# Modulation loads and matmuls in the norm holes of a two-block mixer stack: one unit between the sums and their spreading, eleven units instead of eight behind the mixers

## The chip, the cores and the metric

The kernel runs on one core of a Trainium2 chip. The metric is the device time of one execution in microseconds (us); the time before is the median of three runs. TensorE is called PE, VectorE DVE, ScalarE ACT, GpSimd POOL and SyncE SP.

## What is computed

A stack of two blocks over 256 tokens of width 1024, two layers each, all in float32. Only the parts that the change touches are shown. A layer of the first block is

```python
m = mixer_block(rms_norm(x, norm_mix_pre[layer]), ...)
x = x + rms_norm(m, norm_mix_post[layer])
h = rms_norm(x, norm_ffn_pre[layer])
f = swiglu(h, w_ffn_gate[layer], w_ffn_up[layer], w_ffn_down[layer])
x = x + rms_norm(f, norm_ffn_post[layer])
```

The second block is modulated: for each of its two layers a vector of 6 x 1024 numbers is needed for the latents and another for the context,

```python
mod_x = jax.nn.silu(c) @ ada_w[l] + ada_b[l]
mod_c = jax.nn.silu(c_ctx) @ ada_w[l] + ada_b[l]
```

with `ada_w[l]` of 1024 x 6144. These products depend on nothing that the first block makes, and the kernel computes them while the first block runs.

## The kernel before, in words

**The weight stream.** All weights lie in HBM as units of 128 x 1024 floats (512 KB). SP loads the units of the matrices one after the other into three buffers `raw` (L906, after waiting for `lo_ready` of the unit three before); ACT makes the rounded high part `w_hi` of each unit (L1492) and POOL the rest `w_lo` (L945, two halves), each in four buffers; PE multiplies by both. Products run tile by tile: `product` (L987 to L989), `product_halves` (L1003, L1007) and, for the first two tiles of a stage, `side_by_side` (L1047 to L1050), which takes row tile k of both as soon as `h_ready` tells of row k.

**The modulation units.** `ada_w` of both layers is 96 units of 512 KB, numbered 0 to 95, 48 for each layer. A unit is loaded by `load_modulation` on SP (L915) into one of six buffers (`ADA_SLOTS`), which lie in parts of `spare_lo`, `mix` and `spare_hi` that the first block leaves free. Its load waits for `ada_used` of the unit six before. On PE `modulation_unit` (L1141 to L1153) waits for the unit's load (`ada_loaded`) and does four products of 128 x 2 by 128 x 256 (L1151, eight matmul records, since a float32 product takes two). `ada_places` says at which of the places of a layer of the first block the units stand: at certain tiles of the gates and branches, in the feed-forward part (`FFNS`, 22 pairs of tiles), and in the norms: `MID1` and `PRE1` between the mixer and the feed-forward part, `MID2` and `PRE2` behind the feed-forward part of layer 0. Layer 0 of the first block carries units 0 to 47, layer 1 units 48 to 95. Before the change `MID1` has units 16 to 21 and `PRE1` units 22 and 23 in layer 0, and 68 to 73 and 74, 75 in layer 1.

**The order of the loads.** One list, `LOADS`, built by `load_order`, holds the loads of both kinds for SP's one queue. A modulation load stands where the unit six before it is used. Behind the mixer of layer 0 the list runs: raw units 80 to 90, modulation units 22 to 29, raw unit 91; in layer 1: raw units 233 to 241, modulation units 74 to 81, raw unit 242.

**The norm holes.** Behind the last product of the mixer (`product(y1, 0, SEQ)`) come two norms. `last_rows_sum` sums the squares of the mixer's output over the width on PE (L1090), ACT takes the root (L1544), DVE the reciprocal (L1933), and `spread_inverse` spreads the result over the partitions on PE (L1103, waits for `inv_ready`). DVE then scales and adds to `xs` tile by tile (L2040, L2044), ACT squares each tile (L1521), and `norm_sums` sums these on PE (L1090), again with root, reciprocal and spreading. DVE and ACT then make the normed rows `hl` (L1942, L1550, L1946), and `side_by_side` starts the feed-forward part. In `norm_sums` the units of `MID1` stand as follows: all but three ahead of the sums, and one each behind the sums of tiles 1, 3 and 5. The units of `PRE1` stand behind the spreading.

PE runs its instructions in the order of the program, SP its own likewise: a wait on either holds back all that stands behind it.

Of the kernel before, what the change touches and what calls it, by code (L numbers as in the profile page):

```python
# [19 lines left out]
DEPTH = 2  # L20
# [8 lines left out]
NFF = FF // P  # L29
# [24 lines left out]
POST1, MID1, PRE1 = 3 * KD, 3 * KD + 1, 3 * KD + 2  # L54
FFNS = list(range(3 * KD + 3, 3 * KD + 3 + NFF))
POST2, MID2, PRE2 = FFNS[-1] + 1, FFNS[-1] + 2, FFNS[-1] + 3
# [3 lines left out]
def spread(n, places):  # L60
    out, groups = [0] * N_PLACES, -(-n // ADA_GROUP)
    for i in range(n):
        out[places[i // ADA_GROUP * len(places) // groups]] += 1
    return out


def ada_places(l):

    counts = spread(16 if l < DEPTH - 1 else 20, GATES[4:])
    for place, n in ((MID1, 6), (PRE1, 2)):  # L70
        counts[place] += n
    for place, n in enumerate(spread(16 if l < DEPTH - 1 else 20, FFNS[3:NFF - 3])):
        counts[place] += n
    if l < DEPTH - 1:
        counts[MID2] += 6
        counts[PRE2] += 2
    assert sum(counts) == ADA_LAYER
    at, n = [], l * ADA_LAYER
    for more in counts:
        at.append(list(range(n, n + more)))  # L80
        n += more
    return at


ADA_AT = [ada_places(_l) for _l in range(DEPTH)]
ROWS_AT, TURN_AT, MOD_AT = {}, {}, {}
for _l in range(DEPTH):
# [384 lines left out]
SINGLE1, SINGLE2 = 1, 3  # L472
# [80 lines left out]
def mixer_stack_kernel(nc, stream, vectors, consts, decay, gla_masks, positions, x_in, ctx_in, out):  # L553
# [186 lines left out]
    STAT, X = banks[2], banks[3:8]  # L740
# [150 lines left out]
    with nc.Block() as block:  # L891
# [65 lines left out]
        def _(pe):  # L957
# [13 lines left out]
            def product(x, c0, c1, count=1, fresh=None, late=None, more=1):  # L971

                for i_tile in range(count):
                    t, n, b = TILES[at["tile"]], PLACE.first_out[at["tile"]], PLACE.first_block[at["tile"]]
                    acc = bank_of(n)[:, c0:c1]
                    for k in range(t.k):
                        wait_unit((b + k) // UNIT)  # L980
                        slot, i = (b + k) // UNIT % SPLIT, (b + k) % UNIT
                        wh, wl = w_hi[:, slot, i * P:(i + 1) * P], w_lo[:, slot, i * P:(i + 1) * P]
                        if late and late[1] == k:
                            E.need(late[0])
                        if fresh and i_tile == 0:
                            E.need(fresh, more)
                        nc.tensor.matmul(acc, wh, x[:, 0, k, c0:c1], start=k == 0, stop=False)  # L987
                        nc.tensor.matmul(acc, wh, x[:, 1, k, c0:c1], start=False, stop=False)  # L988
                        last = nc.tensor.matmul(acc, wl, x[:, 0, k, c0:c1], start=False, stop=k == t.k - 1)  # L989
                        if k == t.k - 1:  # L990
                            last.then_inc(tile_done, 1)
                        elif i == UNIT - 1:
                            last.then_inc(unit_used, 1)
                    at["tile"] += 1
# [33 lines left out]
            def keep_busy(acc, count):  # L1028

                for _ in range(count):  # L1030
                    nc.tensor.matmul(acc[:, 0:2 * P], ident, cst[:, 0:2 * P], start=True, stop=True)
# [55 lines left out]
            def token_sums(bank, row, c0, c1, first, last):  # L1087

                for j in range(c0 // P, c1 // P):
                    done = nc.tensor.matmul(bank[:, j * P:(j + 1) * P], row[:, j * P:(j + 1) * P], ones,  # L1090
                                            start=first and j == c0 // P, stop=last, skip_group_check=True)
                return done

            def stat_free():
                if at["stat"]:
                    E.need(std_ready)
                at["stat"] += 1

            def spread_inverse(bank, c0, c1):

                E.need(inv_ready)
                for j in range(c0 // P, c1 // P):
                    last = nc.tensor.matmul(bank[:, j * P:(j + 1) * P], inv_col[:, j:j + 1].to_broadcast([P, P]), ident,  # L1103
                                            start=True, stop=True)
                last.then_inc(inv_spread, 1)

            def last_rows_sum(c0, c1, single):

                E.need(sq_ready)
                stat_free()  # L1110
                token_sums(STAT, work[:, 0, :], c0, c1, True, False)
                for k in range(KD - single, KD):
                    E.need(sq_tile, 1 if k > KD - single else KD - single + 1)
                    last = token_sums(STAT, work[:, k, :], c0, c1, False, k == KD - 1)
                last.then_inc(stat_ready, 1)
                spread_inverse(STAT, c0, c1)

            def norm_sums(c0, c1, bank, units=(), spread_bank=None, spare=0):
                stat_free()
                keep_busy(bank, spare)  # L1120
                for unit in units[:-3]:
                    modulation_unit(unit)
                for k in range(KD):
                    E.need(sq_ready)
                    last = token_sums(bank, work[:, k, :], c0, c1, k == 0, k == KD - 1)
                    if k % 2 and k // 2 < len(units[-3:]):
                        modulation_unit(units[-3:][k // 2])
                last.then_inc(stat_ready, 1)
                spread_inverse(spread_bank or bank, c0, c1)

            def projected(x, l, c0, fresh, next_norm, more=1):

                if l == DEPTH - 1:
                    product_halves(x, c0, T2, KD - 1, fresh=fresh, more=more)
                    product(x, c0, T2)
                else:
                    product(x, c0, T2, KD, fresh=fresh, more=more)
                if next_norm:
                    last_rows_sum(c0, T2, SINGLE2)

            def modulation_unit(unit):  # L1141

                part, k, slot = unit // KD, unit % KD, unit % ADA_SLOTS
                acc = X[1 + part % 3]
                pe.wait_ge(ada_loaded[slot], 16 * (unit // ADA_SLOTS + 1))
                if unit == 0:
                    pe.wait_ge(silu_c_ready, 1)
                if k == 0 and part >= 3:
                    pe.wait_ge(ada_rows_out, part - 2)
                for j in range(4):  # L1150
                    last = nc.tensor.matmul(acc[32 * j:32 * j + 2, 0:ADA_COLS], silu_c[:, k, :], ada_raw[slot][:, j, :],  # L1151
                                            start=k == 0, stop=k == KD - 1)
                last.then_inc(ada_used, 1)  # L1153
# [11 lines left out]
            def modulation_at(l, place):  # L1165
                for unit in ADA_AT[l][place]:
                    modulation_unit(unit)
                if (l, place) in TURN_AT:
                    turn_modulation(TURN_AT[l, place])
# [2 lines left out]
            pe.wait_ge(ones_loaded, 16)  # L1172
            c0, c1 = LAT
            for l in range(DEPTH):
                norm_sums(c0, c1, X[4], ADA_AT[l - 1][MID2] if l else ())
                if l:
                    modulation_at(l - 1, PRE2)
                pe.wait_ge(cst_loaded, 16)
                outs = {}
                for step, i in MIX1:  # L1180
                    if step in ("g", "r", "c", "rg", "gr"):
                        n = {"g": 5, "r": 2, "c": 3, "rg": RH, "gr": GH}[step]
# [6 lines left out]
                    elif step == "diag" or step == "take":  # L1189
# [8 lines left out]
                        for h, j in [(h, j) for i_pair in range(2) for j in range(2) for h in (2 * i_pair, 2 * i_pair + 1)]:  # L1198
# [4 lines left out]
                            k = gqk[rows, 1, h // 2, :] if step == "diag" else k_dec[rows, h // 2, :]  # L1203
                            if step == "take" and i == 0:
                                c, k, q = h // 2 * P, k[:, 0:P], q[:, P:SEQ]
                            else:
                                c, k, q = (h // 2 * 2 + j) * P, k[:, j * P:(j + 1) * P], q[:, j * P:(j + 1) * P]
# [16 lines left out]
                    elif step == "score":  # L1224
                        q, k = rqk[:, i, 0, :], rqk[:, i, 1, :]
# [44 lines left out]
                        modulation_at(l, KD * b + f)  # L1270
                product_halves(y1, 0, SEQ, KD - 1, fresh=merged_ready)
                product(y1, 0, SEQ)
                last_rows_sum(c0, c1, SINGLE1)
                norm_sums(c0, c1, X[4], ADA_AT[l][MID1])
                modulation_at(l, PRE1)
                for t in range(NFF):
                    if t:
# [9 lines left out]
                product(hid, 0, SEQ)  # L1287
                if l == DEPTH - 1:
                    pe.wait_ge(ctx_root, 1)
                last_rows_sum(c0, c1, SINGLE1)  # L1290


            for l in range(DEPTH):
                c0 = 0 if l < DEPTH - 1 else SEQ
# [6 lines left out]
                for step, i in mixer2(l):  # L1301
# [52 lines left out]
                    elif step == "att":  # L1354
# [14 lines left out]
                        if 2 <= i < len(pairs) + 2:  # L1369
                            n = before + i - 2  # L1370
# [60 lines left out]
                    elif step == "acc":  # L1431
                        h, d, n = i
# [1208 lines left out]
```

## Time and profile before

| | |
|---|---|
| median of three runs | 2741.41 us (2739.74 to 2745.48) |
| the profiled execution's own time | 2744.02 us |
| its span (first to last instruction) | 2741.8 us |
| granted TensorE clock, mean | 0.993 |
| PE busy, matmuls | 2661.7 us (97%) |
| PE busy, weight loads | 2272.6 us (83%) |
| DVE, ACT, POOL busy | 1315.5, 1286.7, 1608.9 us |
| HBM read | 382.51 MB, 140 GB/s over the span |

The profiled execution's own time is 2.2 us more than its span, for what lies around the first and the last instruction, and 2.6 us more than the median. A timeline row has its start and its length in us, the engine, the line, the operation, what it writes and reads, how many instructions are merged in it, and in brackets the idle time ahead of it with what ended that. The ends of matmuls are modelled and overlap the next one's start; the pitch from start to start is what PE takes. SPq rows are SP's issues of DMAs, not the transfers. In a view of windows the last three columns are the granted clock as a share of 2.4 GHz, the mean busy share of the 16 DMA engines, and the bytes moved per second.

### The profile page before, as it was taken

The numbers are of one execution on the slowest core, as the hardware profiler recorded it, in microseconds if no ns is written. First come the engines' busy times: TensorE is split into PE (matmuls) and PEld (weight loads), VectorE is DVE, ScalarE is ACT, GpSimd is POOL, SyncE is SP. The second block draws the span as 40 slices with busy tenths as digits, with TensorE's granted clock in tenths as the row PEclk, the third lists the DMA queues.
The fourth block names the chain that finished last, engine by engine and source line by source line (L and its number), as shares of the span: only waits on it lengthen the run. The fifth ranks groups of instructions, "written<-read, shape, count | busy, mean of one in ns | idle before, by whom it ended". The sixth has DMA issues, their size and how long they took to land.

```text
span 2741.8 us, 41593 instructions
## 1 busy us (share of the span) xinstructions
PE 2661.7 (97%) x16136; PEld 2272.6 (83%) x16136; DVE 1315.5 (48%) x2433; ACT 1286.7 (47%) x2042; POOL 1608.9 (59%) x1252
## 2 busy tenths in 40 slices
PE   7999999999999999999999999999999999999999
PEld 7898788888887888786788788888887889998888
DVE  4575533256654343875523424432333855335644
ACT  5464544444645454436434333442343565445644
POOL 5678688767786885432233345444443635457787
PEclk9999999999999999999999999999999999999999
DMA  5357776534686753221121222233222423234455
GB/s 204 116 192 269 230 253 225 162 122 139 229 294 223 261 171 128 82 81 47 52 79 62 77 85 96 81 100 100 93 93 80 143 85 116 93 108 160 158 181 162
DMA packets 144867, 386.12 MB, mean 141 GB/s; under 512 B 11824, under 2 KB 64304, under 8 KB 144688
## 3 DMA queue, kind: packets, MB, share of 16 engines
q1 hardware_dynamic: 144688, 383.61, 42.5%
q8 instruction: 128, 2.10, 0.3%
q14 instruction: 51, 0.42, 0.1%
HBM read 382.51 MB, written 1.05 MB: 140 GB/s over the span
## 4 chain that ended last, share of the span: by engine, by line
POOL 52%; issue 46%; PE 1%; POOLq 1%; DMA 0%; DVE 0%; ACT 0%; DVEq 0%
POOL w_lo L945 52%; PE bank L1003 1%; POOLq L942 0%; PE bank L1007 0%; DMA raw<-stream 0%; POOLq L949 0%; PE bank L989 0%; PE bank L988 0%; PE bank L987 0%; POOLq L945 0%; ACT fc L1903 0%; DVE fc L2591 0%; DVE xs L2326 0%; DVE bank L2603 0%; DVE hid L2606 0%
## 5 line engine op out<-in xcount | busy, mean ns | idle before, releaser
L945 POOL TENSOR_TENSOR w_lo<-raw,w_hi 128x512 fp32r<-128x512 f32 x1248 | 1608.7, 1319 | 1123.0 <-ACT w_hi L1492 1120.4
L1492 ACT ACTIVATE w_hi<-raw 128x1024 fp32r<-128x1024 f32 x624 | 655.0, 1054 | 379.9 <-DMA raw<-stream 170.3
L987 PE MATMUL bank<-hl,w_hi 128*128 128x512 f32 (+1 forms) x2016 | 694.0, 344 | 15.7 <-POOL w_lo L945 11.2
L989 PE MATMUL bank<-hl,w_lo 128*128 128x512 f32 (+1 forms) x2016 | 677.8, 336 | 0.0
L988 PE MATMUL bank<-hl,w_hi 128*128 128x512 f32 (+1 forms) x2016 | 677.7, 336 | 0.0
L987 PEld LDWEIGHTS bank<-hl,w_hi 128*128 128x128 f32 x2016 | 387.3, 192 | 62.7 <-issue 10.3
L988 PEld LDWEIGHTS bank<-hl,w_hi 128*128 128x128 f32 x2016 | 387.6, 192 | 42.0 <-issue 4.4
L989 PEld LDWEIGHTS bank<-hl,w_lo 128*128 128x128 f32 x2016 | 387.1, 192 | 38.3
L1003 PE MATMUL bank<-hl,w_hi 128*128 128x512 f32 x1312 | 344.1, 395 | 2.2 <-POOL w_lo L945 1.9
L1003 PEld LDWEIGHTS bank<-hl,w_hi 128*128 128x128 f32 x1312 | 234.7, 189 | 50.2 <-issue 9.0
L1007 PEld LDWEIGHTS bank<-hl,w_lo 128*128 128x128 f32 x1312 | 181.5, 190 | 16.2 <-DVE hl L2566 2.9
L1007 PE MATMUL bank<-hl,w_lo 128*128 128x256 f32 x1312 | 186.5, 282 | 2.2 <-DVE hl L2566 2.2
L2591 DVE SCALAR_TENSOR_TENSOR fc<-bank,vec,fc 128x510 f32<-128x510 f32 (+1 forms) x88 | 54.2, 616 | 182.2 <-ACT fc L1903 182.1
L2326 DVE SCALAR_TENSOR_TENSOR xs<-bank,mod,xs 128x256 f32<-128x256 f32 x93 | 42.8, 481 | 180.4 <-PE bank L989 132.8
L1003 PE MATMUL bank<-hid,w_hi 128*128 128x512 f32 x462 | 128.0, 397 | 0.0
L1903 ACT ACTIVATE fc<-bank,vec 128x512 f32<-128x512 f32 (+1 forms) x88 | 59.0, 671 | 138.2 <-PE bank L989 108.8
L2381 DVE SCALAR_TENSOR_TENSOR bank<-z,vec,bank 128x512 f32<-128x512 f32 (+1 forms) x232 | 123.0, 612 | 0.0
L1070 PE MATMUL bank<-w_hi,hl 128*128 128x256 f32 x384 | 111.7, 291 | 5.4 <-POOL w_lo L945 5.3
L987 PE MATMUL bank<-y,w_hi 128*128 128x256 f32 (+1 forms) x336 | 110.6, 329 | 2.1 <-DVE y L2560 1.8
L1071 PE MATMUL bank<-w_lo,hl 128*128 128x256 f32 x384 | 109.2, 284 | 0.0
L1072 PE MATMUL bank<-w_hi,hl 128*128 128x256 f32 x384 | 109.2, 284 | 0.0
L989 PE MATMUL bank<-y,w_lo 128*128 128x256 f32 (+1 forms) x336 | 108.7, 324 | 0.0
(327 smaller groups left out, 3998.3 us busy)
## 6 DMA issues: line engine op xcount, KB each, us to landing
raw<-stream SPq DMA_DIRECT2D x624, 512.0 KB, 3.4
spare_lo<-stream SPq DMA_DIRECT2D x32, 512.0 KB, 5.8
mix<-stream SPq DMA_DIRECT2D x32, 512.0 KB, 5.9
spare_hi<-stream SPq DMA_DIRECT2D x32, 512.0 KB, 5.8
xs<-x_rows SPq DMA_DIRECT2D x4, 256.0 KB, 4.1
xs<-ctx_rows SPq DMA_DIRECT2D x1, 1024.0 KB, 14.5
out_rows<-xs SPq DMA_DIRECT2D x8, 128.0 KB, 2.8
dec<-decay SPq DMA_DIRECT2D x1, 768.0 KB, 11.0
```

The source lines that it names most:

```text
L945: last = nc.gpsimd.tensor_tensor(w_lo[:, unit % SPLIT, part], raw[:, unit % RAW, part], w_hi[:, unit % SPLIT, part], ALU.subtract)
L987: nc.tensor.matmul(acc, wh, x[:, 0, k, c0:c1], start=k == 0, stop=False)
L988: nc.tensor.matmul(acc, wh, x[:, 1, k, c0:c1], start=False, stop=False)
L989: last = nc.tensor.matmul(acc, wl, x[:, 0, k, c0:c1], start=False, stop=k == t.k - 1)
L1003: return nc.tensor.matmul(acc[:, :], w, x[:, :, k, c0:c1], start=k == 0, stop=k == t.k - 1)
L1007: return nc.tensor.matmul(acc[:, 0:SEQ], w, x[:, 0, k, c0:c1], start=False, stop=False)
L1070: nc.tensor.matmul(acc, h_hi[:, k, c:c + P], wh, start=k == 0, stop=False)
L1071: nc.tensor.matmul(acc, h_hi[:, k, c:c + P], wl, start=False, stop=False)
L1072: last = nc.tensor.matmul(acc, h_lo[:, k, c:c + P], wh, start=False, stop=k == t.k - 1)
L1492: nc.scalar.activation(w_hi[:, n % SPLIT, :], raw[:, n % RAW, :], ACT.Copy).then_inc(hi_ready, 1)
L1903: nc.scalar.activation(fc[:, t % 2, j, cols], rows, ACT.Identity, bias=v_("ffn_conv_b_2", l, i), scale=v_("ffn_conv_w_2", l, 2 * NFF + i)) ...
L2381: C.do(V.scalar_tensor_tensor(out, z, w, y, MUL, ADD))
```

## The change

The places `MID1` and `PRE1` get eight and three units instead of six and two, and the last places of the feed-forward part three fewer in each layer. One unit of `MID1` (and of `MID2`) moves up into `last_rows_sum`, between the sums and the spreading; one of them moves behind the last sum of `norm_sums`, again between the sums and the spreading. Three units still stand between the sums of `norm_sums`, the rest ahead of them.

```diff
@@ def ada_places(l):
     counts = spread(16 if l < DEPTH - 1 else 20, GATES[4:])
-    for place, n in ((MID1, 6), (PRE1, 2)):
+    for place, n in ((MID1, 8), (PRE1, 3)):
         counts[place] += n
-    for place, n in enumerate(spread(16 if l < DEPTH - 1 else 20, FFNS[3:NFF - 3])):
+    for place, n in enumerate(spread(13 if l < DEPTH - 1 else 17, FFNS[3:NFF - 3])):
         counts[place] += n
@@
-            def last_rows_sum(c0, c1, single):
+            def last_rows_sum(c0, c1, single, units=()):
...
                 last.then_inc(stat_ready, 1)
+                for unit in units:
+                    modulation_unit(unit)
                 spread_inverse(STAT, c0, c1)
 
             def norm_sums(c0, c1, bank, units=(), spread_bank=None, spare=0):
                 stat_free()
                 keep_busy(bank, spare)
-                for unit in units[:-3]:
+                for unit in units[:-4]:
                     modulation_unit(unit)
                 for k in range(KD):
                     E.need(sq_ready)
                     last = token_sums(bank, work[:, k, :], c0, c1, k == 0, k == KD - 1)
-                    if k % 2 and k // 2 < len(units[-3:]):
-                        modulation_unit(units[-3:][k // 2])
+                    if k % 2 and k // 2 < len(units[-4:-1]):
+                        modulation_unit(units[-4:-1][k // 2])
                 last.then_inc(stat_ready, 1)
+                for unit in units[-1:]:
+                    modulation_unit(unit)
                 spread_inverse(spread_bank or bank, c0, c1)
@@
-                norm_sums(c0, c1, X[4], ADA_AT[l - 1][MID2] if l else ())
+                norm_sums(c0, c1, X[4], ADA_AT[l - 1][MID2][1:] if l else ())
@@
-                last_rows_sum(c0, c1, SINGLE1)
-                norm_sums(c0, c1, X[4], ADA_AT[l][MID1])
+                last_rows_sum(c0, c1, SINGLE1, ADA_AT[l][MID1][:1])
+                norm_sums(c0, c1, X[4], ADA_AT[l][MID1][1:])
                 modulation_at(l, PRE1)
@@
-                last_rows_sum(c0, c1, SINGLE1)
+                last_rows_sum(c0, c1, SINGLE1, ADA_AT[l][MID2][:1])
```

By the same functions the units then stand so. Layer 0: `MID1` has units 16 to 23 (16 in `last_rows_sum`, 17 to 19 ahead of the sums, 20, 21 and 22 between them, 23 behind them) and `PRE1` units 24 to 26; the group of four at the 16th pair of feed-forward tiles shrinks to one unit (39). Layer 1: `MID1` has 68 to 75, `PRE1` 76 to 78, and the last group is unit 95 alone. The list of loads has modulation units 22 to 32 between raw units 90 and 91, and 74 to 84 between raw units 241 and 242. `MID2` keeps units 40 to 45: 40 in `last_rows_sum`, 41 ahead, 42 to 44 between, 45 behind.

## Rows read from the trace of the kernel before

**Rows 1.** The page: busy time by engine, and the chain that ended last

```profile
PE 2661.7 (97%) x16136; PEld 2272.6 (83%) x16136; DVE 1315.5 (48%) x2433; ACT 1286.7 (47%) x2042; POOL 1608.9 (59%) x1252
...
POOL 52%; issue 46%; PE 1%; POOLq 1%; DMA 0%; DVE 0%; ACT 0%; DVEq 0%
```

**Rows 2.** Timeline of PE, norm holes behind the mixer, layer 0

```profile
318.14 1.35 PE L1090 MATMUL bank<-cst,work 128*128 128x128 f32 x8
320.04 0.71 PE L1103 MATMUL bank<-cst,sd 128*128 128x128 f32 x4 [0.55 <-DVE sd L1933]
320.68 1.04 PE L1151 MATMUL bank<-spare_hi,silu_c 128*2 128x256 f32 x16
...
327.14 0.61 PE L1151 MATMUL bank<-mix,silu_c 128*2 128x256 f32 x8
327.69 1.16 PE L1090 MATMUL bank<-cst,work 128*128 128x128 f32 x8
329.46 0.71 PE L1103 MATMUL bank<-cst,sd 128*128 128x128 f32 x4 [0.62 <-DVE sd L1933]
330.10 1.04 PE L1151 MATMUL bank<-spare_hi,silu_c 128*2 128x256 f32 x16
332.07 0.47 PE L1048 MATMUL bank<-hl,w_hi 128*128 128x512 f32 x1 [0.92 <-DVE hl L1946]
```

**Rows 3.** Timeline of PE, a group of four units, feed-forward part of layer 0

```profile
428.23 1.04 PE L1151 MATMUL bank<-spare_lo,silu_c 128*2 128x256 f32 x16
429.10 1.05 PE L1151 MATMUL bank<-mix,silu_c 128*2 128x256 f32 x16
```

**Rows 4.** Timeline of SP's issues around the norm holes, layer 0

```profile
302.55 19.53 SPq L906 DMA_DIRECT2D raw<-stream  x8
322.12 1.22 SPq L915 DMA_DIRECT2D spare_hi<-stream  x2
323.39 1.70 SPq L915 DMA_DIRECT2D spare_lo<-stream  x2
326.18 2.17 SPq L915 DMA_DIRECT2D mix<-stream  x2
```

**Rows 5.** DMA issues in windows at 322.12, 323.39 and 326.18: us to landing

```profile
spare_hi<-stream SPq DMA_DIRECT2D x1, 512.0 KB, 5.7
...
spare_lo<-stream SPq DMA_DIRECT2D x1, 512.0 KB, 8.8
...
mix<-stream SPq DMA_DIRECT2D x1, 512.0 KB, 9.0
```

**Rows 6.** Timeline of PE, the same holes, layer 1

```profile
850.78 0.61 PE L1151 MATMUL bank<-spare_lo,silu_c 128*2 128x256 f32 x8
...
853.10 0.71 PE L1103 MATMUL bank<-cst,sd 128*128 128x128 f32 x4 [0.62 <-DVE sd L1933]
...
855.75 0.47 PE L1048 MATMUL bank<-hl,w_hi 128*128 128x512 f32 x1 [0.96 <-DVE hl L1946]
```

**Rows 7.** Timeline of SP's issues, layer 1

```profile
845.00 1.22 SPq L915 DMA_DIRECT2D mix<-stream  x2
...
849.82 2.17 SPq L915 DMA_DIRECT2D spare_lo<-stream  x2
```

**Rows 8.** DMA issues in windows at 845.00 and 849.82: us to landing

```profile
mix<-stream SPq DMA_DIRECT2D x1, 512.0 KB, 6.6
...
spare_lo<-stream SPq DMA_DIRECT2D x1, 512.0 KB, 7.8
```

**Rows 9.** Windows: busy of PE, PEld, DVE, ACT, POOL; PEclk, DMA share, GB/s

```profile
324.00:327.50 3.50, 3.50 (x40) 2.15 (x32) 2.70 (x8) 2.00 (x5) 0.00 (x0) 1.00 0.82 228
...
328.00:337.00 9.00, 7.46 (x56) 5.99 (x55) 6.07 (x17) 4.97 (x11) 0.41 (x1) 1.00 1.09 355
...
588.00:595.00 7.00, 4.95 (x31) 4.66 (x28) 6.83 (x8) 2.64 (x6) 6.69 (x4) 0.77 0.24 76
```

**Rows 10.** Timeline of PE: the gap ahead of the clock's fall

```profile
591.84 0.58 PE L1070 MATMUL bank<-w_hi,hl 128*128 128x256 f32 x1 [2.05 <-POOL w_lo L945]
```

## The prediction

> **What bounds the kernel now.** First the page: PE is busy 97% of the span, and the chain that ended last runs over POOL and issue [rows 1], which is an average over stages and says nothing of the one that changes. So I read the timeline of PE from the mixer's last sums to the first feed-forward matmul. In layer 0 PE stands still at four places that the rows show or imply: 0.55 us ahead of the first spreading, 0.62 us ahead of the second, both for DVE's reciprocal, 0.92 us ahead of the feed-forward part for the first normed rows, and a shorter one ahead of the second sums [rows 2]. Layer 1 looks the same, 0.62 and 0.96 us [rows 6]. Everywhere else around the change PE is in a row of matmuls without a gap: in the feed-forward part the group of four units stands between products, and what it takes is paid in full [rows 3]. So this stage is PE's, and the holes are DVE's and ACT's.
>
> Then SP's issues and their landings, since the moved units have loads that move with them. Behind the mixer raw loads go out until 302.55 + 19.53 = 322.08, then modulation units 22 and 23, from 323.39 units 24 and 25, from 326.18 units 26 and 27 [rows 4]. Unit 22 lands 5.7 us after its issue, at 327.8; unit 24 8.8 us after, at 332.2; unit 26 9.0 us after, at 335.2 [rows 5]. In layer 1 unit 74 goes out at 845.00 and lands at 851.6, unit 78 at 849.82 and lands at 857.6 [rows 7, 8]. These transfers are slow because they queue: from 328 to 337 the DMA engines are busy all the time and move 355 GB/s [rows 9], so a load of 524 KB takes 1.48 us of them.
>
> **The change part by part.**
>
> *Three units fewer in the feed-forward part of each layer.* Two units start 0.87 us before the next two [rows 3]: 0.435 us a unit. The group shrinks from four to one, so 3 x 0.435 = 1.31 us a layer, 2.61 us in all, paid in full because PE has no gap there. The group stays, and with it what it costs to go from products to units and back.
>
> *A unit between the mixer's sums and their spreading.* The hole is 0.55 us by the modelled end of the sums [rows 2]. The unit fills 0.435 us of it, and unit and spreading change over in about 0.1 us (a unit's start at 327.14 to the next sums at 327.69 is 0.55 us [rows 2]). It just fits: cost 0. It was loaded long before (its load waits for a unit used in the gates). If the cover fails it costs up to 0.435 us.
>
> *A unit behind the second sums.* The hole is 0.62 us [rows 2, 6], the same fit, cost 0 by PE. The same holds for the two holes behind layer 0's feed-forward part, where six units are only put elsewhere: 0, bound 0.435 us each.
>
> *The third unit in PRE1.* The hole ahead of the feed-forward part is 0.92 us [rows 2], so by PE it costs 0 too.
>
> *The loads.* This is the term that decides. Of the eleven units only six are loaded before the hole. Before, the two units loaded inside it (22, 23) stood at 330.10, behind the second spreading. Now units 22 to 26 are loaded inside it and all used before the feed-forward part. That unit 16 is used earlier brings nothing forward: unit 22's issue at 322.12 stands directly behind a raw load [rows 4]. Units 25 and 26 do go out earlier, some 0.6 and 1.7 us, since the units six before them are used sooner, but they queue behind 22 to 24.
> - Unit 22 is wanted at 327.14 and lands at 327.8: the sums of the last two tiles start 0.7 us late. In layer 1 unit 74 is wanted at 850.78 and lands at 851.6, 0.8 us late [rows 6 to 8]. Both are covered by what follows.
> - Unit 24 is wanted at 330.8 (the spreading at 330.2 by then) and lands at 332.2; 26 lands at 335.2. PE has then one unit left, 0.435 us, and some 0.15 us of wait and changeover, so the feed-forward part starts at 335.75 instead of 332.07: 3.7 us late. All eight normed rows are then ready or nearly so, which gives back 0.1 us: 3.6.
> - Layer 1: unit 78 lands at 857.6, the part starts at 858.2 instead of 855.75: 2.45 us late, 2.35 with what is given back.
> - The DMA engines are busy 0.82 of 324 to 327.5 [rows 9]; if the earlier issues filled all the rest, 0.18 x 3.5 = 0.6 us would be won in each layer. I take half, 0.3 each, between the ends 0 and 0.6, as the packets already queued should fill most of it.
>
> So the waits cost 3.6 + 2.35 - 0.6 = 5.35 us. Their lower end, if no load were late, is 0.
>
> A rule speaks for a cheaper wait. The row has 355 GB/s. The Trainium skill, "DMA: Bandwidth & Descriptors", section Bandwidth, has 425 GB/s for large reads from HBM with one core busy, and its Specifications put line rate at pieces of 512 bytes and up. By it a load would take an estimated 1.23 us, units 26 and 78 would land near 332.8 and 856.5, and the change would come out at about -0.2 us instead. This case's trace disagrees for these loads, and I go by it.
>
> *Queued behind the waits.* On PE the whole feed-forward part. On SP the loads of units 27 to 32 and then raw unit 91, which now stands behind three more modulation loads, 3 x 1.48 = 4.4 us of transfer. PE's own start is 3.7 us later, and raw 91 is wanted only at the fourth pair of tiles; I take 0, and up to 1 us if ACT and POOL then run late.
>
> **Sum.** -2.61 + 5.35 = +2.7 us. The profiled execution took 2744.02 us and would take 2746.7; its span of 2741.8 would be 2744.5. It lies 2.6 us over the median, so the median goes from 2741.41 to 2744.1, 0.1% slower. A measurement of this kernel tells 0.2%, 5.5 us, from no change, and not less.
>
> **Rivals.**
>
> *A, the loads come in time.* If landings follow the issues and not the queue, the five loads are there when wanted. For it: they are issued sooner, and other modulation loads land in less (5.7 us for unit 22). Against it: the engines' share of 1.09 from 328 on [rows 9], and unit 24, issued at 323.39 in both kernels, lands at 332.2 in any case. Time: -2.6 us, 2738.8; with only layer 1's loads in time about 2741.7.
>
> *B, slower: the clock falls in the stall.* In the hole of layer 0 PE would wait three times between 330.6 and 335.2, up to 1.5 us each, with units of 0.435 us between. Elsewhere in this trace a gap of 2.05 us [rows 10] stands beside a window of 7 us with a granted clock of 0.77 [rows 9]: (1 - 0.77) / 0.5 x 7 = 3.2 us at 1.2 instead of 2.4 GHz, 1.6 us lost. Against it: no single wait reaches 2.05 us, and the clock is 1.00 in both windows of layer 0 now [rows 9]. If it falls in both layers the sum is 2.7 + 3.2 = +5.9 us, 2747.3; twice as long a stretch in each gives +9.1, 2750.5. It decides from the point where PE's stall is seen with a granted clock under 1.
>
> *C, the units between sums and spreading aren't covered.* The margins are about 0.1 us. Where the DMAs rule (the second sums of both layers) it doesn't matter; at the other four holes it costs up to 4 x 0.435 = 1.7 us: +4.4, 2745.8. It is also how the change could fail to do what it says, to fill idle time.
>
> **How the numbers follow.** Forecast 55%, A 24%, B 10%, C 8%, something else 3%. The range goes from A, less 1 us for the spread of medians, to between the two sizes of B: 2737.8 to 2748.8. Faster by over 0.2% needs more than A gives: 4%. Slower by over 0.2% is B and a sum of C, late raw loads and the upper end of the waits: 13%. The rest, 83%, is within 0.2%.
>
> **What would show it.** Right: in the timeline of PE, units 24 to 26 (and 76 to 78) apart from each other by over 1 us each, with idle time ended by DMA, the first L1048 at about 335.5 and 858, and groups of one unit at the last feed-forward place; the issue-to-landing of units 24 to 26 still near 9 us; the spreading at 320.0 unmoved. Wrong: L1048 at 332 with no DMA wait (A), a granted clock under 1 in 330 to 345 (B), the first spreading later than 320.1 (C), or a new wait for POOL in the first four pairs of the feed-forward part (raw 91).

## The result, and the profile after

| | before | changed |
|---|---|---|
| median | 2742.89 us (12 runs) | 2745.95 us (12 runs) |
| lowest to highest | 2739.74 to 2745.48 | 2741.3 to 2750.36 |
| ratio, 95% interval | | 1.0016 (1.0009 to 1.0024) |

By the ratio the changed kernel is 0.16% slower, 4.4 us, with an interval of 2.5 to 6.6 us; the two medians of the table differ by 3.1 us. The forecast was 2744.1 us, 0.10% slower, and most likely too little to tell from no change. The time lies in the range of the forecast, and the direction is the forecast's. The loss stays under the 0.2% that the forecast took as the least that can be told from nothing, but the interval of these twelve runs excludes 1, so it is told all the same. The profiled execution happened to be the fastest of the twelve (2741.3 us, span 2739.1), so its span says nothing against the one of before; what follows compares stretches, not spans.

The page of the changed kernel, busy time and chain, against [rows 1]:

```profile
PE 2661.8 (97%) x16136; PEld 2269.9 (83%) x16136; DVE 1320.4 (48%) x2433; ACT 1285.6 (47%) x2042; POOL 1610.1 (59%) x1252
...
POOL 49%; issue 45%; PE 4%; POOLq 1%; DVE 1%; ACT 0%; DMA 0%; DVEq 0%; ACTq 0%
```

The same work, as it must be; the page as a whole can't show a change of this size. The timeline of PE, changed kernel, behind the mixer of layer 0, answers to [rows 2] (L1155 is `modulation_unit`, L1151 before):

```profile
318.72 1.35 PE L1090 MATMUL bank<-cst,work 128*128 128x128 f32 x8
320.62 0.71 PE L1103 MATMUL bank<-cst,sd 128*128 128x128 f32 x4
...
327.71 0.61 PE L1155 MATMUL bank<-spare_hi,silu_c 128*2 128x256 f32 x8
328.25 1.16 PE L1090 MATMUL bank<-cst,work 128*128 128x128 f32 x8
329.34 0.61 PE L1155 MATMUL bank<-spare_hi,silu_c 128*2 128x256 f32 x8
330.03 0.71 PE L1103 MATMUL bank<-cst,sd 128*128 128x128 f32 x4
330.91 0.61 PE L1155 MATMUL bank<-spare_lo,silu_c 128*2 128x256 f32 x8 [0.17 <-DMA spare_lo<-stream]
332.43 0.61 PE L1155 MATMUL bank<-spare_lo,silu_c 128*2 128x256 f32 x8 [0.91 <-DMA spare_lo<-stream]
333.92 0.61 PE L1155 MATMUL bank<-mix,silu_c 128*2 128x256 f32 x8 [0.88 <-DMA mix<-stream]
334.47 0.50 PE L1048 MATMUL bank<-hl,w_hi 128*128 128x512 f32 x1
```

Read it from the start of the sums. The first spreading stands 320.62 - 318.72 = 1.90 us behind, as before (320.04 - 318.14), the second 11.31 us against 11.32: the two new units there are covered. Then units 24, 25 and 26 come one by one, 1.5 us apart, each ended by a DMA. The first feed-forward matmul stands 15.75 us behind the sums instead of 13.93. Layer 1, same view, against [rows 6]:

```profile
855.63 0.61 PE L1155 MATMUL bank<-spare_hi,silu_c 128*2 128x256 f32 x8 [0.86 <-DMA spare_hi<-stream]
857.56 0.65 PE L1155 MATMUL bank<-spare_lo,silu_c 128*2 128x256 f32 x8 [1.31 <-DMA spare_lo<-stream]
858.14 0.79 PE L1048 MATMUL bank<-hl,w_hi 128*128 128x512 f32 x1
858.73 0.41 PE L1050 MATMUL bank<-hl,w_lo 128*128 128x256 f32 x1
```

The sums start at 842.17 here: 15.97 us instead of 13.97. The last two rows show a second thing. L1048 takes 0.79 us where [rows 2] have 0.47, and L1050 0.41 us, where it took 0.28 before. In windows of the changed and then of the old kernel (columns as in [rows 9]):

```profile
855.00:867.00 12.00, 10.05 (x60) 8.03 (x61) 6.97 (x19) 6.40 (x12) 2.52 (x2) 0.86 1.02 332
```

```profile
855.00:867.00 12.00, 11.25 (x64) 9.93 (x65) 7.49 (x19) 8.39 (x14) 6.10 (x5) 1.00 0.64 205
```

The granted clock is 0.86 instead of 1.00: (1 - 0.86) / 0.5 x 12 = 3.4 us at 1.2 GHz, right behind the stall. That is rival B, in one layer.

SP's issues and the landing of the last load, changed kernel, against [rows 4, 5] (unit 26 in the third row, its landing in the last):

```profile
321.50 1.22 SPq L915 DMA_DIRECT2D spare_hi<-stream  x2
322.76 1.40 SPq L915 DMA_DIRECT2D spare_lo<-stream  x2
325.12 2.65 SPq L915 DMA_DIRECT2D mix<-stream  x2
```

```profile
mix<-stream SPq DMA_DIRECT2D x1, 512.0 KB, 8.8
```

It goes out at 325.12, 6.40 us behind the sums instead of 8.04, and lands 8.8 us later, at 333.9, which is when PE's unit begins. Unit 22 goes out earlier as well in this execution, 321.50 - 318.72 = 2.78 us behind the sums instead of 3.98. The group at the last feed-forward place is one unit now, against [rows 3]:

```profile
430.68 0.61 PE L1155 MATMUL bank<-mix,silu_c 128*2 128x256 f32 x8
431.22 0.50 PE L1003 MATMUL bank<-hl,w_hi 128*128 128x512 f32 x1
```

### The profile page after: what moved, and what is told of

Its sections match the earlier page's. It is cut to its first block, busy times and chain, and to the rows that moved or that the text cites. A ratio compares the mean times of both kernels' runs of the same rounds, so it can differ in the third digit from the quotient of the medians.

```text
span 2739.1 us, 41594 instructions
## 1 busy us (share of the span) xinstructions
PE 2661.8 (97%) x16136; PEld 2269.9 (83%) x16136; DVE 1320.4 (48%) x2433; ACT 1285.6 (47%) x2042; POOL 1610.1 (59%) x1252
## 4 chain that ended last, share of the span: by engine, by line
POOL 49%; issue 45%; PE 4%; POOLq 1%; DVE 1%; ACT 0%; DMA 0%; DVEq 0%; ACTq 0%
POOL w_lo L945 49%; PE bank L1003 3%; PE bank L1007 1%; POOLq L942 0%; ACT fc L1907 0%; DVE fc L2595 0%; ACT w_hi L1496 0%; DMA raw<-stream 0%; POOLq L949 0%; DVE bank L2588 0%; PE bank L989 0%; PE bank L988 0%; PE bank L987 0%; DVE bank L2607 0%; DVE fc L2597 0%
## 6 DMA issues: line engine op xcount, KB each, us to landing
xs<-ctx_rows SPq DMA_DIRECT2D x1, 1024.0 KB, 14.2
```

## The experiments

A measurement tells some 0.1% here, 2 to 3.5 us, and the terms are of that size. So each run was read in two ways: the ratio, and four stretches of its one profiled execution, each the difference of two starts in the timeline of PE, within 0.01 us. A **hole** runs from the mixer's last sums (L1090 x8) to the first L1048; a **feed-forward part** from there to the next L1090. The column "sum" adds the four differences to the kernel before, in us. The last column says where a stretch at half clock begins and how long it is. Each ratio is to the kernel before in the same comparison. The line numbers of a kernel with added lines are one to three higher.

| kernel | holes, layers 0, 1 | feed-forward, 0, 1 | sum | ratio (95%) | half clock behind a hole |
|---|---|---|---|---|---|
| before | 13.93, 13.97 | 193.65, 197.60 | 0 | 1 | none |
| changed | 15.75, 15.97 | 192.42, 197.37 | +2.4 | 1.0016 (1.0009 to 1.0024) | 858.0, 3.4 us |
| e5, changed again | 16.64, 17.23 | 192.34, 198.19 | +5.3 | 1.0022 (1.0013 to 1.0031) | 857.8, 6.8 us |
| e12, changed, third | 16.82, 17.12 | 192.40, 198.18 | +5.4 | 1.0020 (1.0011 to 1.0030) | 860.7, 6.8 us |
| e1, order alone | 13.93, 13.92 | 193.66, 197.59 | 0.0 | 1.0004 (0.9994 to 1.0014) | none |
| e2, nine units | 13.92, 13.92 | 193.17, 196.83 | -1.3 | 1.0002 (0.9991 to 1.0013) | none |
| e4, five loads left out | 13.95, 13.92 | 192.33, 195.86 | -3.1 | 0.9996 (0.9986 to 1.0005) | none |
| e6, thirteen units | 20.76, 19.84 | 193.56, 195.98 | +11.0 | 1.0032 (1.0020 to 1.0044) | 340.3 and 866.0, 6.8 us each |
| e7, filled with three | 17.47, 17.95 | 192.41, 195.61 | +4.3 | 1.0013 (1.0004 to 1.0022) | none |
| e10, filled with one | 17.80, 16.77 | 192.37, 195.92 | +3.7 | 1.0004 (0.9993 to 1.0015) | none |
| e3, loads earlier | 14.01, 13.92 | 192.43, 195.89 | -2.9 | 0.9998 (0.9985 to 1.0011) | none |
| e8, the same again | 14.13, 13.92 | 192.32, 195.85 | -2.9 | 0.9997 (0.9988 to 1.0006) | none |
| e11, the same, third | 13.92, 15.88 | 192.34, 199.46 | +2.5 | 0.9985 (0.9975 to 0.9996) | none (one at 1033.4) |

**e1: the order alone.** The changed code with the old numbers:

```diff
-    for place, n in ((MID1, 8), (PRE1, 3)):
+    for place, n in ((MID1, 6), (PRE1, 2)):
-    for place, n in enumerate(spread(13 if l < DEPTH - 1 else 17, FFNS[3:NFF - 3])):
+    for place, n in enumerate(spread(16 if l < DEPTH - 1 else 20, FFNS[3:NFF - 3])):
```

> The changed order (one unit between the sums and the spreading of each norm, the rest as changed) with the old numbers: six units in MID1, two in PRE1, sixteen and twenty in the feed-forward parts. Theory W (the change loses by waits for modulation loads in the hole, and the new places of the units cost nothing): the stretch from the mixer's last sums to the first L1048 matmul stays at 13.9 us in both layers, the first spreading stays 1.90 us behind the start of the sums, and the time is that of the kernel before within 1 us (ratio 0.9997 to 1.0004). Rival C (units between sums and spreading aren't covered): each spreading 0.1 to 0.4 us later, and up to 2 us longer in all.

All four stretches are those of before within 0.05 us, and the spreadings stand at 1.90 and 11.32 us. The two holes behind the feed-forward part of layer 0 are unmoved too: from the sums there to the first product of the next mixer it is 13.92 us before, 13.92 in e1 and 13.93 in the changed kernel. Units between sums and spreading cost nothing, and alone bring nothing either. Rival C is out.

**e2: nine units.** `MID1` seven, `PRE1` two, fifteen and nineteen in the feed-forward parts.

> The changed order with nine units in the hole: seven in MID1, two in PRE1, fifteen and nineteen in the feed-forward parts. Theory W: the last unit of the hole is the third that is loaded inside it, which lands about when it is wanted (at most 0.3 us late), so the stretch from sums to first L1048 is 13.9 to 14.3 us, one unit less is paid in each feed-forward part, 0.87 us in all, and the time is 0.3 to 0.9 us under the kernel before (ratio 0.9996 to 1.0000). If what slows the changed kernel lies elsewhere than in the fourth and fifth of these loads, it is still 1 us or more over.

No wait for a load in the hole, and 0.48 and 0.77 us less in the feed-forward parts: -1.3 us in the stretches. Its ratio of 1.0002 can't be told from 1, nor from the 0.9996 to 1.0000 expected. So the loss begins with the tenth and the eleventh unit.

**e4: the loads left out.** It leaves out the loads of units 22 to 26 and 74 to 78; these units multiply by old data.

```diff
+UNLOADED = [u for l in range(DEPTH) for u in (ADA_AT[l][MID1] + ADA_AT[l][PRE1])[ADA_SLOTS:]]
...
             def load_modulation(unit):
+                if unit in UNLOADED:
+                    return
...
-                pe.wait_ge(ada_loaded[slot], 16 * (unit // ADA_SLOTS + 1))
+                pe.wait_ge(ada_loaded[slot], 16 * len([u for u in range(slot, unit + 1, ADA_SLOTS) if u not in UNLOADED]))
```

> The changed kernel without the loads of the five units that are used inside the hole beyond the six buffers (22 to 26 and 74 to 78): they are left out, and these units multiply by what the buffer holds from the unit six before, so the modulation is not the reference's. Nothing else is changed. Theory W: PE has no wait for a load in the hole, the stretch from sums to first L1048 is 13.9 to 14.0 us, and the time is the kernel before less the three units a layer, -2.6 us (ratio 0.9988 to 0.9993). Rival C: 0.4 to 1.7 us of it is lost at the spreadings. Rival B (the clock falls): with no stall no fall at 320 to 345 or 855 to 870. If the kernel stays above the one before, the loads are not the cause.

The timeline of PE of this kernel, end of the hole of layer 0:

```profile
332.40 0.71 PE L1106 MATMUL bank<-cst,sd 128*128 128x128 f32 x4
333.04 1.04 PE L1158 MATMUL bank<-spare_lo,silu_c 128*2 128x256 f32 x16
333.90 0.61 PE L1158 MATMUL bank<-mix,silu_c 128*2 128x256 f32 x8
335.04 0.47 PE L1051 MATMUL bank<-hl,w_hi 128*128 128x512 f32 x1 [0.52 <-DVE hl L1953]
```

All three units of `PRE1` fit, and PE still waits 0.52 us for DVE's rows: the third unit is paid by idle time, as forecast. The stretches give -3.1 us. All that the changed kernel has over that hangs on these ten loads, the transfers and the waits together; the ratio of 0.9996 agrees in direction, though its interval reaches 1.0005, and it misses the 0.9988 to 0.9993 expected.

**e5 and e12: the changed kernel again.**

> The changed kernel once more, unchanged: a second profile of the same program. Theory W: the stretches from the mixer's last sums to the first L1048 are again 15.7 and 16.0 us within 0.3, since the landings repeat, and the ratio is within 1.0005 to 1.0020. Theory B (the stalls let the clock fall in many executions, as the first profile has it at 858.0): a stretch at half clock again begins between 330 and 340 or 855 and 865. If neither layer has one, the fall at 858.0 was chance, as those elsewhere in every profile.

> The changed kernel a third time: a third profile of its stretches and of the clock behind them. Theory W with B: stretches between 15.7 and 17.3 us, a half clock behind at least one of the two holes, ratio to the kernel before 1.0010 to 1.0025.

The holes don't repeat within 0.3 us, as was expected for e5: they are 16.6 to 17.2 us in these two, and e5's ratio lies just over the expected range. What does repeat is the clock: it falls at the end of the hole of layer 1 in all three profiles, never at that of layer 0. The timeline of PE of e12, layer 1:

```profile
857.33 0.61 PE L1155 MATMUL bank<-spare_hi,silu_c 128*2 128x256 f32 x8
859.98 0.61 PE L1155 MATMUL bank<-spare_hi,silu_c 128*2 128x256 f32 x8 [2.03 <-DMA spare_hi<-stream]
861.48 1.03 PE L1155 MATMUL bank<-spare_lo,silu_c 128*2 128x256 f32 x8 [0.89 <-DMA spare_lo<-stream]
862.45 0.80 PE L1048 MATMUL bank<-hl,w_hi 128*128 128x512 f32 x1
```

A gap of 2.03 us, unit 77, a gap of 0.89 us, and unit 78 takes 1.03 us instead of 0.61: it runs at half clock already. The granted clock falls at 860.7, within the second of these gaps. The window of this kernel has 0.74:

```profile
855.00:867.00 12.00, 9.00 (x58) 5.76 (x59) 6.08 (x17) 5.79 (x11) 2.52 (x2) 0.74 1.09 351
```

In the first profile gaps of 0.86 and 1.31 us were enough; in layer 0 those of 0.17, 0.91 and 0.88 us were not, nor those of 1.08, 0.89 and 0.88 us in e5, nor those of 0.85, 0.25, 0.89 and 0.89 us in e12.

**e6: thirteen units.** `PRE1` has five, the feed-forward parts eleven and fifteen.

> The changed kernel with two more units in PRE1 of both layers (thirteen in the hole) and two fewer in each feed-forward part: the suspected cost doubled. Theory W: each of the two waits for a landing 1.5 us behind the one before, so the stretches grow by 2 x 1.5 = 3.0 us to 18.7 and 19.0 us, each feed-forward part gets 0.87 us shorter, and the time is 4.2 us over the changed kernel: ratio to the kernel before 1.0022 to 1.0035. Theory B: a fall of the clock at 330 to 345 or 855 to 870 in this profile, too. If the stretch grows by only 0.9 us, the units are paid and not the landings.

The timeline of PE, end of the hole of layer 0:

```profile
336.40 0.61 PE L1155 MATMUL bank<-spare_lo,silu_c 128*2 128x256 f32 x8 [0.89 <-DMA spare_lo<-stream]
337.89 0.61 PE L1155 MATMUL bank<-mix,silu_c 128*2 128x256 f32 x8 [0.88 <-DMA mix<-stream]
339.39 0.61 PE L1155 MATMUL bank<-mix,silu_c 128*2 128x256 f32 x8 [0.89 <-DMA mix<-stream]
340.91 1.03 PE L1155 MATMUL bank<-spare_hi,silu_c 128*2 128x256 f32 x8 [0.91 <-DMA spare_hi<-stream]
341.88 0.80 PE L1048 MATMUL bank<-hl,w_hi 128*128 128x512 f32 x1
```

Each further unit adds a full landing, 1.5 us from start to start, not its own 0.435. The holes are 5.0 and 3.9 us longer than in the first profile of the changed kernel where 3.0 was expected, 4.4 and 3.1 longer than the mean of the three; in each a load was late as well (PE waits 1.06 us for unit 23 and 2.32 us for unit 78). Here the clock falls in layer 0 as well, at 340.3, within the last of the four gaps of 0.9 us.

**e7 and e10: PE kept at work in the waits.** Idle products, three (1.5 us) or one (0.43 us), ahead of the second and the third unit of `PRE1`:

```diff
-                for unit in ADA_AT[l][place]:
+                for n_unit, unit in enumerate(ADA_AT[l][place]):
+                    if place == PRE1 and n_unit:
+                        keep_busy(STAT, 3)
                     modulation_unit(unit)
```

> The changed kernel with three idle products (identity times constants, 128 x 256, into the STAT bank, which nothing reads there) ahead of the second and the third unit of PRE1, so that PE works in part of its waits. Theory W alone: the landings still rule, the stretches stay at 15.7 and 16.0 us within 0.2, and the time is the changed kernel's. Theory B: no half clock begins between 330 and 345 or 855 and 870, and the time is up to 1.5 us under the changed kernel for each layer in which it fell.

> As the kernel with three idle products, but with one, 0.43 us instead of 1.5 us ahead of the second and the third unit of PRE1, so that the filling is shorter than the waits of 0.9 us there and can't hold the units back. The landings still rule the stretch: 15.7 to 17.3 us in each layer. Theory B (the gaps in PE's work let the clock fall): with half of each gap filled the clock falls less often, none or one half-clock stretch behind the two holes, and the time is 0.5 to 2.5 us under the changed kernel's. If the filling of three helped only by chance, this is the changed kernel's time.

Neither has a half clock behind a hole, in either layer. The window of e10 in layer 1:

```profile
855.00:867.00 12.00, 10.52 (x74) 7.42 (x73) 7.54 (x19) 6.47 (x12) 2.53 (x2) 1.00 1.09 351
```

The timeline of PE of e10, layer 0, shows that one product leaves a wait and so holds nothing back:

```profile
334.91 0.61 PE L1155 MATMUL bank<-spare_lo,silu_c 128*2 128x256 f32 x8 [0.26 <-DMA spare_lo<-stream]
335.45 0.70 PE L1031 MATMUL bank<-cst 128*128 128x256 f32 x2
336.41 0.61 PE L1155 MATMUL bank<-mix,silu_c 128*2 128x256 f32 x8 [0.26 <-DMA mix<-stream]
336.95 0.50 PE L1048 MATMUL bank<-hl,w_hi 128*128 128x512 f32 x1
```

Its feed-forward part of layer 1 is 195.92 us against 197.37 to 198.19 in the changed kernel: 1.5 to 2.3 us saved by doing more work, in a hole of 16.77 us, which lies between the changed kernel's 15.97 and 17.23. Its hole of layer 0, 17.80 us, is over the 15.7 to 17.3 expected: there PE waited 0.74 us for unit 22 and 1.23 us for unit 23, ahead of any filling, and the second spreading stands 13.27 us behind the sums instead of 11.32. With three products the holes grow (17.47 and 17.95): three products and a unit take 2.04 us, from the unit at 332.84 to the one at 334.88, where the landings are 1.5 us apart. So e7's expectation of unmoved stretches missed. By the ratios both lie under the changed kernel measured beside them (1.0013 against 1.0022, 1.0004 against 1.0020), but the intervals overlap. The traces show it in one profile each; the granted clocks of all executions, below, bear it out.

**e3, e8 and e11: the five loads ahead of raw units 89 and 90.** The version that the findings point to. Raw units 89 and 90 aren't wanted before the third pair of feed-forward tiles, yet stand ahead of unit 22 in SP's queue.

```diff
-            order.append((used[i - ADA_SLOTS] if i >= ADA_SLOTS else first, 1, l * ADA_LAYER + i))
+            behind = l * ADA_LAYER + i in ADA_AT[l][MID1] + ADA_AT[l][PRE1] and i >= ADA_SLOTS and used[i - ADA_SLOTS] == at(POST1)
+            order.append((used[i - ADA_SLOTS] - 2 * behind if i >= ADA_SLOTS else first, 1, l * ADA_LAYER + i))
```

> The changed kernel, eleven units, with one thing moved: in the list of loads the five modulation loads that the hole itself needs stand ahead of the last two raw units instead of behind them. Theory W: the first of them goes out about 1.3 us earlier, and 2 x 1.3 us of raw transfers are behind them instead of ahead, so the last lands 3 to 4 us earlier than in the changed kernel, near or before the time when it is wanted: the stretch from sums to first L1048 falls from 15.8 to 14.0 to 14.5 us in both layers, and the time is 1.5 to 2.5 us under the kernel before (ratio 0.9991 to 0.9995). If the raw units, now later, are wanted soon after, POOL's low parts of units 89 and 90 end late and part of it comes back as a wait of L1003 for POOL in the second or third pair of feed-forward tiles. Rival (transfers are not what decides): no change against the changed kernel, ratio near 1.0015.

> The kernel with the five modulation loads ahead of the last two raw units, once more, on the chip of this comparison beside the changed kernel. Theory W: the stretches are again 13.9 to 14.1 us, the feed-forward parts 192.4 and 195.9 us, 2.9 us in all under the kernel before, and 3 to 4 us under the changed kernel of the same job: ratio to the kernel before 0.9985 to 1.0000.

> The kernel with the five modulation loads ahead of the last two raw units, a third time, to narrow its interval: stretches 13.9 to 14.2 us, no half clock behind the holes, ratio to the kernel before 0.9988 to 1.0000.

SP's issues of e8, layer 0, and then the timeline of PE of e8 at the end of that hole:

```profile
318.39 0.33 SPq L907 DMA_DIRECT2D raw<-stream  x1
322.25 1.81 SPq L916 DMA_DIRECT2D spare_hi<-stream  x2
324.10 1.30 SPq L916 DMA_DIRECT2D spare_lo<-stream  x2
326.70 0.54 SPq L916 DMA_DIRECT2D mix<-stream  x1
327.28 1.40 SPq L907 DMA_DIRECT2D raw<-stream  x2
```

```profile
332.25 1.04 PE L1156 MATMUL bank<-spare_lo,silu_c 128*2 128x256 f32 x16
333.88 0.61 PE L1156 MATMUL bank<-mix,silu_c 128*2 128x256 f32 x8 [0.59 <-DMA mix<-stream]
334.43 0.50 PE L1049 MATMUL bank<-hl,w_hi 128*128 128x512 f32 x1
```

The first load now follows the use of unit 16, 1.95 us behind the sums (320.30) instead of 2.78, 3.11 and 3.88 in the three profiles of the changed kernel, and raw units 89 and 90 go out behind unit 26. The wait for POOL in the second or third pair of tiles, which e3's expectation allowed for, isn't there. The hole is 14.13 us, with 0.59 us of wait for unit 26 that stands almost wholly in time that PE would have idled anyway. It is under 14.2 us in five of the six holes of the three profiles. In the sixth, e11's layer 1, unit 78 landed late again:

```profile
856.76 0.61 PE L1156 MATMUL bank<-spare_lo,silu_c 128*2 128x256 f32 x8 [2.33 <-DMA spare_lo<-stream]
```

So the margin is thin, and e11's expectation of 13.9 to 14.2 us missed there. (The long feed-forward part of that profile has a half clock at 1033.4 behind a wait of 1.75 us for POOL, far from the hole and not seen in the others.) Against the changed kernel measured beside it this version is clearly faster: 0.9997 (0.9988 to 1.0006) beside 1.0022 (1.0013 to 1.0031), and 0.9985 (0.9975 to 0.9996) beside 1.0020 (1.0011 to 1.0030). Against the kernel before, the stretches of e3 and e8 say -2.9 us, 0.11%; the three ratios are 0.9998, 0.9997 and 0.9985, and only the third has its interval under 1. The first misses the 0.9991 to 0.9995 expected. It is likely faster than the kernel before, too, but that isn't shown.

## Why the prediction was right, and where its size was off

**The gain.** Forecast -2.61 us. The feed-forward parts without a fall of the clock are 192.4 and 195.9 us: -1.25 and -1.7, -2.95 in all. The pitch of 0.435 us holds. Where the 0.4 us more in layer 1 come from isn't shown. PE waits 0.72 us for POOL there before and 0.29 us in the changed kernel, but e1 has 0.29 us of it as well, and its part is as long as before (197.59).

**The units between sums and spreading.** Forecast 0; where no load is late the spreadings are unmoved, and e1 shows it alone. Right.

**The third unit in PRE1.** Forecast 0 by PE; e4 has it within the hole with 0.52 us to spare. Right.

**The waits.** Forecast 5.35 us for both layers. The holes of the three profiles of the changed kernel are 2.47 us longer on the mean in layer 0 (1.82, 2.71, 2.89) and 2.80 in layer 1 (2.00, 3.26, 3.15): 5.3 us. The sum fits; the parts less so, and that their errors cancel is luck. Layer 0 was taken at 3.3 and layer 1 at 2.05, because I took the landings of one execution for what repeats. They move by over a microsecond between executions, and [rows 4, 5] have a late one themselves: from unit 22 to 24 it is 332.2 - 327.8 = 4.4 us, from 24 to 26 only 3.0, two loads each. Unit 26's landing was put at 17.0 us behind the sums, or 0.3 less; it came at 15.2, 16.1 and 16.3 in the three profiles, 0.8 to 1.8 us earlier instead of 0.3. Unit 78 came at 15.4, 16.3 and 16.2, where before it was 15.8. So the 0.3 us for the earlier issues was too little in layer 0, and in layer 1 a late load outweighed it in two of three. That the queue rules and not the issue was right: units 26 and 78 went out some 1.6 us earlier in relation to the sums in all three, and the gain in their landing was anything from 1.8 us to -0.4. Without a late load each landed 1.5 us behind the one before it.

The prediction's other estimate, 1.23 us a load from the 425 GB/s of the Trainium skill, "DMA: Bandwidth & Descriptors", section Bandwidth, is not borne out. The Trainium skill has that rate for a transfer of 16 MB; these are loads of 512 KB. Where no load is late, the units behind the waits start 1.5 us apart in every profile, and more where one is late.

**What is queued behind.** Forecast 0 for raw unit 91: there is no wait of PE for POOL in the first pairs of feed-forward tiles in any profile. Right.

**The clock.** This is the term that was mis-sized: "Against it: no single wait reaches 2.05 us", and 0 in the sum, 10% as a rival. In all three profiles of the changed kernel the clock fell at the end of the hole of layer 1 and cost 1.5, 2.3 and 2.3 us (197.37, 198.19 and 198.18 against 195.9), 2.0 on the mean. (The prediction looked for it in 330 to 345, in layer 0, where it didn't come.) Rival B had priced one fall at 1.6 us, so its price was about right and its chance too low. The argument took one gap by itself; PE had several, with units of 0.435 us between them, and the pair 0.86 and 1.31 sufficed. And in two of the three profiles one wait was 2.03 us long, since a landing came late.

The profiles are one execution each, but the mean granted clock is on record for every execution, 11 or 12 of a kernel. Where e5, e7 and e8 were measured together it is 0.9925 for the changed kernel, 0.9941 with three idle products and 0.9935 with the loads earlier; where e12, e10 and e11 were, it is 0.9922, 0.9938 with one idle product and 0.9932 with the loads earlier. Each of these means is good to about 0.0003. The changed kernel is thus 0.0010 under the same units with the loads earlier, which over 2741 us is 0.0010 / 0.5 x 2741 = 5.5 us more at half clock, near the 3.4, 6.8 and 6.8 us of its profiles. So the fall repeats, and it goes with the waits. The kernels in which these waits are gone or nearly so (e1 to e4, e8, e11) also lie 0.0002 to 0.0008 under the kernel before of their comparison, 1 to 4 us at half clock; why is open, and it may be why the ratios of e3 and e4 gain less than their stretches.

Together: -2.95 + 5.3 + 2.0 = +4.3 us on the mean of three profiles, against +2.7 forecast; the ratios of 1.0016, 1.0022 and 1.0020 say 4.4 to 6.0 us. Up to 1.7 us between the stretches and the ratios is open; it is within the intervals. That e1, e2 and e4 have no such stretches and no such ratios says that the loss isn't in the order of the units.

The cause was as forecast: six buffers feed a hole that asks for eleven units, and the other five arrive at the pace of the queue, not of PE. The likeliest mechanism and a part of rival B came true together. The time fell in the range although one term was put at 0, since the range reached up to rival B.

## What to carry to other kernels

Idle time of an engine is worth as much work as can be fed in it: before filling a hole, count what is already on the chip and what must land inside it, and price each further piece at the spacing of the landings (1.5 us here), not at its own time (0.435 us). Ask what stands ahead of these loads in their queue, and whether it is wanted sooner. And where PE is left with short waits between short pieces of work, add what the clock takes back in the dense work behind them.

## What the runs showed of the hardware that I had not expected

The granted TensorE clock went to half behind PE's gaps of 0.86 and 1.31 us with one unit of 0.435 us between them (first profile, 858.0), and within the last of four gaps of 0.88 to 0.91 us (e6, 340.3), but not after gaps of 0.17, 0.91 and 0.88 us (first profile, layer 0) or 1.08, 0.89 and 0.88 us (e5, layer 0). A single wait of 2.33 us, longer than any of these, left it at full (e11, layer 1). Filling 0.43 us of the gaps ahead of the last two units was enough to keep it up in the one profile made so. What exactly decides it is open.

The landing of one and the same modulation load moves from execution to execution: unit 78, which went out 6.41 us behind the sums in all three profiles of the changed kernel, was used 15.4, 16.3 and 16.2 us behind them, and its hole was 15.97, 17.23 and 17.12 us. The load that comes late differs (unit 77 in two, 78 in one), and what stands behind it is late with it.
